# Four GpSimd sums moved behind the placed blocks, and one weight split moved from GpSimd to VectorE, in a two-block transformer kernel on one core

## The reference

```python
mod = silu(c) @ w_ada[l] + b_ada[l]            # the "side sums": 6 groups of 1024 columns
proj = h @ w_in[l]                             # dn_qkv, dn_z, sw_q, sw_k, sw_v, gate_a, gate_b, ...
...
L = where(tri_strict, einsum(k_beta, kc) * decay, 0)       # chunks of tokens, 8 heads
sol = triangular_solve(L + eye, rhs, lower=True, unit_diagonal=True)
u, w = sol[..., :Dv], sol[..., Dv:]
... scan over chunks: v_new = u - w S ; o = q S + (q k^T decay) v_new ; S = S exp(g) + k^T v_new
o_dn = rms_norm(o_dn) * silu(dn_z)
y_b  = swa_sink_attention(partial_rope(sw_q), partial_rope(sw_k), sw_v)
```

## Time and profile before

| what | value |
|---|---|
| median of three runs | 2323.31 us (2321.83 to 2323.89) |
| the profiled execution | 2324.14 us, its span 2322.4 us |
| mean granted TensorE clock | 0.969 of full speed |
| TensorE busy with matmuls | 2186.8 us (94%) |
| VectorE busy | 1556.9 us (67%) |
| ScalarE busy | 1075.1 us (46%) |
| GpSimd busy | 559.7 us (24%) |

### The profile page before, as it was taken

One profiled execution on the slowest core, in us unless ns is written; L12 is line 12 of the kernel. 1 busy time (PEld: TensorE's weight loads), 2 busy tenths in 40 slices (PEclk: granted clock), 3 DMA queues, 4 the chain that ended last, 5 costly groups with the idle time before them and its releaser, 6 DMA issues.

```text
span 2322.4 us, 39767 instructions
## 1 busy us (share of the span) xinstructions
PE 2186.8 (94%) x17241; PEld 2096.0 (90%) x17241; DVE 1556.9 (67%) x1870; ACT 1075.1 (46%) x1398; POOL 559.7 (24%) x264
## 2 busy tenths in 40 slices
PE   7996899999999869999999999989999999989999
PEld 7986889899989768899999999869999999878999
DVE  6869666777678777667667556786556555786554
ACT  2564464433456535634345344544445344535333
POOL 0856003799346530348000000000000000000000
PEclk7998999999999979999999999999999999989999
DMA  9752055677657213366555555325555556424553
GB/s 285 248 166 73 19 164 164 198 257 236 219 164 235 88 40 113 124 218 207 191 177 170 183 186 177 115 85 164 183 189 173 183 186 189 133 73 137 190 182 127
DMA packets 332855, 383.79 MB, mean 165 GB/s; under 512 B 12551, under 2 KB 315402, under 8 KB 332554
## 3 DMA queue, kind: packets, MB, share of 16 engines
q1 hardware_dynamic: 332234, 381.10, 51.1%
q10 hardware_dynamic: 448, 0.16, 0.0%
HBM read 380.19 MB, written 1.05 MB: 164 GB/s over the span
## 4 chain that ended last, share of the span: by engine, by line
PE 77%; DVE 13%; ACT 6%; issue 3%; DMA 0%; SPq 0%; ACTq 0%; DVEq 0%
PE bank L727 16%; PE bank L728 16%; PE bank L729 16%; PE bank L956 5%; PE bank L958 5%; PE bank L957 5%; DVE weights_low L1348 4%; ACT weights_high L2074 3%; PE bank L741 1%; DVE arena L1454 1%; PE bank L1002 1%; PE bank L1132 1%; DVE arena L1761 1%; PE bank L1147 1%; PE bank L765 1%
## 5 line engine op out<-in xcount | busy, mean ns | idle before, releaser
L1348 DVE TENSOR_TENSOR weights_low<-ring,weights_high 128x2048 fp32r<-128x2048 f32 x300 | 742.2, 2474 | 436.6 <-ACT weights_high L2074 436.3
L727 PE MATMUL bank<-h_high,weights_high 128*128 128x256 f32 x3296 | 946.8, 287 | 22.5 <-DVE weights_low L1348 13.7
L728 PE MATMUL bank<-h_low,weights_high 128*128 128x256 f32 x3296 | 929.9, 282 | 0.0
L729 PE MATMUL bank<-h_high,weights_low 128*128 128x256 f32 x3296 | 929.1, 282 | 0.0
L2074 ACT ACTIVATE weights_high<-ring 128x2048 fp32r<-128x2048 f32 x302 | 578.1, 1914 | 706.6 <-PE bank L729 544.9
L727 PEld LDWEIGHTS bank<-h_high,weights_high 128*128 128x128 f32 x3296 | 624.7, 190 | 39.1 <-DVE weights_low L1348 21.6
L728 PEld LDWEIGHTS bank<-h_low,weights_high 128*128 128x128 f32 x3296 | 625.8, 190 | 3.7 <-issue 3.6
L729 PEld LDWEIGHTS bank<-h_high,weights_low 128*128 128x128 f32 x3296 | 625.4, 190 | 0.0
L956 PE MATMUL bank<-hidden_high,weights_high 128*128 128x256 f32 x1056 | 299.0, 283 | 1.2 <-DVE hidden_low L1594 0.8
L957 PE MATMUL bank<-hidden_low,weights_high 128*128 128x256 f32 x1056 | 298.4, 283 | 0.0
L958 PE MATMUL bank<-hidden_high,weights_low 128*128 128x256 f32 x1056 | 298.4, 283 | 0.0
(11 more groups left out here) (427 smaller groups left out, 2928.9 us busy)
## 6 DMA issues: line engine op xcount, KB each, us to landing
ring<-in_w_in SPq DMA_DIRECT2D x80, 1024.0 KB, 5.3
ring<-in_w_up SPq DMA_DIRECT2D x44, 1024.0 KB, 5.2
ring<-in_ffn_w_gate SPq DMA_DIRECT2D x44, 1024.0 KB, 5.3
ring<-in_ffn_w_up SPq DMA_DIRECT2D x44, 1024.0 KB, 5.4
ring<-in_ffn_w_down SPq DMA_DIRECT2D x44, 1024.0 KB, 4.9
side<-in_w_ada SPq DMA_DIRECT2D x42, 1024.0 KB, 7.8
ring<-in_w_down SPq DMA_DIRECT2D x22, 1024.0 KB, 5.0
ring<-in_w_dn_out SPq DMA_DIRECT2D x8, 1024.0 KB, 5.2
```

Source lines behind the costliest of these rows:

```text
L727: mm(o[:, m, :], a_, high[:, t, :], start=(t == 0), stop=False)
L728: mm(o[:, m, :], a_, low[:, t, :], start=False, stop=False)
L729: last = mm(o[:, m, :], b_, high[:, t, :], start=False, stop=(t == KT - 1))
L1348: v.tensor_tensor(low, wide(q), high.bitcast(F32), ALU.subtract).then_inc(chunk_split, 1)
```

## The change

GpSimd's list: the four side sums 6 to 9 stand together behind a wait for the four placed quarters of the blocks, and the split of z3 is gone from it. VectorE's list: it makes that split itself, behind `rope_turned_in(2)`; `rope_turned_in(1)` now stands ahead of `rope_norm(2)`, and `rope_norm(3)` stands behind `rows(1)`.

```diff
@@ VectorE, layer l
                 split(SI["z", l, 0] + 3)
+                rope_turned_in(1)
                 rope_norm(2)
-                rope_turned_in(1)
-                rope_norm(3)
-                split_elsewhere(("z", l, 3))
@@
                 rows(0)
                 rows(1)
+                rope_norm(3)
                 rope_turned_in(2)
+                split(SI["z", l, 3] + 1)
                 exponents(2)
                 exponents(3)
@@ GpSimd
                 g_.memset(Y[:, :, :, :], 0.0).then_inc(y_zeroed, 1)
-                side_sum(6 + 24 * l)
-                n = SI["z", l, 3]
-                q = Q[SPLIT[n]]
-                pool.wait_ge(chunk_rounded, n + 1)
-                high, low = halves(n)
-                g_.tensor_tensor(low, wide(q), high.bitcast(F32), ALU.subtract).then_inc(chunk_split, 1)
-                for j in range(7 + 24 * l, 10 + 24 * l):
+                pool.wait_ge(y_updated, 16 * l + 4)
+                for j in range(6 + 24 * l, 10 + 24 * l):
                     side_sum(j)
```

More of the change, by code:

```diff
@@ L1349, in split @@
                     made[0] += 1
-            def split_elsewhere(key):
-                made[0] = SI[key] + 1
             def modulate(n):
```

## The result

The changed kernel takes 2291.22 us in the median of four runs (2286.71 to 2297.82); four runs of the kernel before beside them give 2322.57 (2320.02 to 2323.89). The ratio is 0.9869, with an interval of 0.9843 to 0.9894: 31.4 us, or 1.3%, faster, where 39.0 were predicted (2284.3). The time lies inside the range of 2279 to 2300, but at the far end of the forecast's own 2280 to 2292. The profiled execution is the one of 2291.59 us, span 2289.8; what follows is read from it.

What follows compares the result with a forecast made beforehand. TensorE, busy for 94%, bounds the kernel; the gain lies where it stands. 20.5 less 1.0 gives 19.5 us a layer, 39.0 for both: 2284.3 against 2323.31, range 2280 to 2292, or 2279 to 2300 with rivals.

Steps and rivals of the forecast that it cites:

- The mechanism: VectorE's chain pays for every operation that reads SBUF alone while GpSimd works on SBUF, nothing for one reading a bank.
- The first part: Stage up to z1's end: the 3.13 us wait at L1089 goes, z1 ends at about 186 instead of 190.76.
- The clock's rival: One chunk a layer runs at TensorE's lower clock behind pauses: 5.8 us a layer, 2296 in all; chance 12%.
- The fourth part: TensorE's and VectorE's arms up to L1119: levels start between 215.1 and 217.8, taken as 216.4, 20.5 us sooner.
- The second part: z3's split on VectorE: it stands 2.2 us for ScalarE's rounded half, splits in 2.3, goes on at 192.7.
- The term `rope_turned_in(3)`: Behind L1119, its two operations reading SBUF alone meet the moved sums: cost 1.0 us a layer, bounds 0 and 3.2.
- Copies from banks: Rival: VectorE's copies from banks into SBUF also wait beside GpSimd's sums, 10 us a layer, 2304; chance 7%.
- bank readers: Rival: all VectorE operations reading banks wait beside the sums, slower by 9.5 us a layer, 2342; chance 3%.
- SyncE's queue and GpSimd's squares: Rival: the moved sums hold SyncE's load queue or GpSimd's squares, 2 to 5 us a layer, about 2292; chance 4%.

Runs made afterwards that it cites:

- sums_as_fills: Kernel before with side sums 6 to 9 replaced, at the same places, by GpSimd zero fills as long that read nothing: 2289.10 us, ratio 0.9854.
- sums_only: Kernel before with only the side sums moved behind the placed blocks, z3's split left on GpSimd: 2288.72 us, ratio 0.9850.
- sums_later: Changed kernel with the side sums waiting for all twelve updates of Y, behind the levels, instead of the placed blocks: 2306.69 us, ratio 0.9926.
- split_late: Changed kernel with z3's split on VectorE moved behind `rows(3)`: 2283.05 us, ratio 0.9824.
- pause_filled: Changed kernel with parts of TensorE's `prepared(0)` and `prepared(1)` run in its pause at L815, around piece 3's sum of rope squares: 2287.19 us, ratio 0.9848.
- split_only: Changed kernel with the side sums left in their old place without their wait, z3's split on VectorE: 2320.93 us, ratio 0.9995.

## Why the prediction was right, and where it was off

**The mechanism was right, its wording too wide.** VectorE's operations with two SBUF inputs, and its copies within SBUF, stand while GpSimd works on the sums. With the sums gone they are clean in both layers (L1755 at most 220 ns), and sums_as_fills shows that a GpSimd which only writes doesn't hold the two-input ones. But I wrote "every VectorE operation that reads SBUF alone". The stream transpose L1750 reads SBUF alone, and in the kernel before it ran inside a side sum (L2516, 217.32 to 218.61) at the 0.71 us that its twin takes after the change with no sum beside it:

```profile
217.42 0.71 DVE L1750 STREAM_TRANSPOSE arena<-arena 128x512 f32<-128x512 f32 x1
```

L1119 came 17.8 us earlier in layer 0 (219.15 for 236.95), 18.5 in its own stretch.

**The first part was mis-sized: it took the products after L815 at full clock.** I reckoned z1's end at "about 186". The first product behind z1 starts at 188.07. The stage started 0.7 us later than before (171.84 for 171.15). In sums_only, where the products behind the pause run fast, the time from z2's split to that product is 186.78 - 172.18 = 14.60 us; in the changed kernel 188.07 - 171.84 = 16.23: 1.6 us. I had priced the clock as a rival at one whole chunk, 5.8 us a layer; it came in two smaller pieces, and this one I had not named.

**The fourth part named the second piece and took its middle.** I allowed `kv_turn(1)` and `kv_turn(2)` 0.9 or 1.8 us each. From `kv_turn(1)` to z3's first product the changed kernel takes 207.34 - 204.47 = 2.87 us and sums_only 204.74 - 203.01 = 1.73; z3 itself takes 6.25 (213.59 - 207.34) and 5.76. That is 1.6 us again. Together 47.31 - 3.3 = 44.0, which is what sums_later, the changed kernel but for the sums' wait, measures (44.06). So the predicted 45.25 (216.4 - 171.15) lay between the two forms, and the change got the slow one: 2.1 us a layer.

**The second part was right in its mechanism, and its edit was worth nothing.** The wait (2.30 for 2.2) and the split (2.29 for 2.3) came as forecast. But I never priced the alternative of leaving the split on GpSimd: 3.2 us of stall for 4.6 of waiting and splitting. sums_only is as fast, and split_late shows what the place cost: 7.2 us, about half of it slow products behind the waits for the rows.

**The term `rope_turned_in(3)` was too small in layer 1.** I took 1.0 with bounds 0 and 3.2; it cost 1.2 in layer 0 and 4.0 in layer 1. The VectorE side was sized well (two long operations, some 1.8 us of excess in layer 0, 2.7 in layer 1). What was missing is TensorE's side: I wrote that TensorE doesn't wait for the copies of L1814 behind them. It did, for 1.15 and 2.13 us at L1190, where the kernel before had no wait, and the longer one was followed by sixteen products in 3.47 us.

**Sum.** In the two profiled executions: gain 18.5 + 18.5, loss 1.2 + 4.0, 0.7 for the later start; 18.5 + 18.5 - 1.2 - 4.0 - 0.7 = 31.1, and with 1.5 at the end of the span (1433.85 - 1432.39) 32.6 = 2322.4 - 2289.8. The 1.5 us are not explained.

**The rivals.** Copies from banks and bank readers don't wait: L1769 691 to 693 ns and L1810 681 to 692 in both layers. SyncE's queue and GpSimd's squares kept 28 and 12.8 us of cover. The clock's rival was the real one, at about half its price (3.3 us a layer for 5.8).

**Left open.** Why the clock behind the same 2.16 us pause is granted in full in one layer and not in the other was not found; it may also be what spreads the changed kernel's runs over 11 us, which no run here shows. What pause_filled is worth in the time is below what these runs tell apart.

## What to carry to other kernels

When VectorE and GpSimd share a stage, sort VectorE's operations by where their inputs lie, and put GpSimd's reading work beside the stretch whose operations read banks: four sums of 8.3 us cost 18.5 us of stall and lost clock in one place and 1 to 4 in the next. Thinning such a stretch was not enough here (split_only); it had to be emptied. And price a wait that you add against the stall that it replaces: the split's move was worth nothing, until it stood where TensorE was just about to want it.

## What the runs showed of the hardware beyond the forecast

- A GpSimd instruction that only writes leaves VectorE's two-input operations alone (56 of them at 153 to 219 ns beside fills in sums_as_fills), but VectorE's tensor_scalar and copies from SBUF to SBUF grew beside it (0.43 to 1.97 us; two copies 1.19 to 3.37).
- How long an operation is held doesn't depend on its own size, but on what is left of GpSimd's operation: 8 elements a partition took 2.19 us (clean 0.17; it ends at 264.75 in sums_later, GpSimd's L2511 at 264.73), 26 took 2.21 (clean 0.19; it ends at 225.81, L2515 at 225.77), and 512 took 2.28 (clean 0.69). So a chain of tiny operations loses the most for its work.
- GpSimd is held too, by the one that came first (3.29 us for 1.27 beside ga0's split in sums_later), and is faster without VectorE in its way: the products of L2510 take 3.74 us for two at 219.08, and 5.79 in the kernel before.
- Behind one and the same pause of 2.16 us TensorE's granted clock was 1.00 in some layers and near its lower level (0.57 in the mean of the window) in others, eight stages of sixteen each; it costs 1.6 us a stage.
